# Big on-chip buffers at multiples of 512 bytes, and a matrix of ones kept as one column

## What is computed

```python
def swiglu(h, w_gate, w_up, w_down):
    return (jax.nn.silu(h @ w_gate) * (h @ w_up)) @ w_down

for l in range(DEPTH):                       # first model
    h = rmsnorm(x, norm_mix[l])
    x = x + (even_mixer(h, ...) if l % 2 == 0 else odd_mixer(h, ...))
    h = rmsnorm(x, norm_ffn[l])
    x = x + swiglu(h, ffn_w_gate[l], ffn_w_up[l], ffn_w_down[l])
for l in range(DEPTH):                       # second model
    x = layer_norm(alpha * x + 0.5 * swiglu_2(x, w_ff1_in[l], w_ff1_out[l]), ...)
    mix = hybrid_mixer(x, ...)               # three attention branches and gates
    x = layer_norm(alpha * x + mix, ...)
    x = layer_norm(alpha * x + 0.5 * swiglu_2(x, w_ff2_in[l], w_ff2_out[l]), ...)
```

## Time and profile before

| | us |
|---|---|
| median of 3 runs (2305.82 to 2306.01) | 2305.96 |
| the profiled execution | 2305.82 |
| its span, first to last instruction | 2304.0 |
| PE busy | 2285.6 |
| DVE busy | 1783.4 |
| ACT busy | 1286.9 |

### The profile page before, as it was taken

The page is one execution under the profiler, slowest core; times in us unless marked ns, Lnnn a source line. Parts: engine busy times, 40 slices in busy tenths (PEclk is TensorE's granted clock), DMA queues, the critical chain, the costliest instruction groups (busy, mean ns, idle before and its releaser), DMA issues.

```text
span 2304.0 us, 37657 instructions
## 1 busy us (share of the span) xinstructions
PE 2285.6 (99%) x15127; PEld 2064.6 (90%) x15127; DVE 1783.4 (77%) x2709; ACT 1286.9 (56%) x2017; POOL 80.0 (3%) x96
## 2 busy tenths in 40 slices
PE   8999999999999999999999999999999999999998
PEld 7988889998888888999999888988889999998887
DVE  6989658779858876797679886698767976798854
ACT  6855455655445554585656554455445856565542
POOL 0022000002100000020000000000000200000000
PEclk9999999999999999999999999999999999999999
DMA  6455565456556556554455555566565543556563
GB/s 229 139 189 191 189 210 169 150 162 205 181 176 211 192 185 192 199 181 134 120 182 185 192 189 180 178 192 202 184 195 192 185 138 120 178 183 214 187 182 99
DMA packets 115452, 412.45 MB, mean 179 GB/s; under 512 B 12880, under 2 KB 14800, under 8 KB 115024
## 3 DMA queue, kind: packets, MB, share of 16 engines
q1 hardware_dynamic: 114992, 407.96, 54.5%
q0 software_dynamic: 288, 2.10, 0.3%
HBM read 408.96 MB, written 1.05 MB: 178 GB/s over the span
## 4 chain that ended last, share of the span: by engine, by line
PE 95%; DVE 4%; ACT 1%; issue 1%; DMA 0%; SPq 0%; DVEq 0%; ACTq 0%
PE ps L441 93%; DVE wlo L2015 1%; PE ps L714 0%; DMA raw<-in_ew_c 0%; DVE RX L2207 0%; DVE x L2067 0%; PE ps L962 0%; ACT region L1476 0%; DVE x L2214 0%; ACT whi L1255 0%; PE ps L1078 0%; DVE R L2225 0%; DVE x L2167 0%; DVE R L2194 0%; DVE x L2266 0%
## 5 line engine op out<-in xcount | busy, mean ns | idle before, releaser
L441 PE MATMUL ps<-xx,whi 128*128 128x512 f32 (+1 forms) x4504 | 1218.1, 357 | 3.6 <-DVE wlo L2015 1.8
L2015 DVE TENSOR_TENSOR wlo<-raw,whi 128x1024 fp32r<-128x1024 f32 (+3 forms) x772 | 925.6, 1207 | 270.7 <-ACT whi L1255 269.3
L1255 ACT ACTIVATE whi<-raw 128x1024 fp32r<-128x1024 f32 (+3 forms) x772 | 801.2, 1044 | 534.9 <-PE ps L441 521.8
L441 PEld LDWEIGHTS ps<-xx,wlo 128*128 128x128 f32 x3696 | 696.5, 188 | 127.4 <-DVE wlo L2015 0.2
L441 PE MATMUL ps<-xx,wlo 128*128 128x256 f32 x3696 | 796.9, 279 | 0.0
L441 PEld LDWEIGHTS ps<-xx,whi 128*128 128x128 f32 x4504 | 696.9, 189 | 8.9 <-issue 4.9
L441 PE MATMUL ps<-H,whi 128*128 128x512 f32 (+1 forms) x2144 | 538.2, 339 | 0.4 <-DVE H L2038 0.4
L441 PE MATMUL ps<-H,wlo 128*128 128x256 f32 x1632 | 363.8, 279 | 0.0
L441 PEld LDWEIGHTS ps<-H,wlo 128*128 128x128 f32 x1632 | 306.5, 188 | 46.8
L441 PEld LDWEIGHTS ps<-H,whi 128*128 128x128 f32 x2144 | 329.3, 188 | 1.8 <-issue 1.1
L2010 DVE TENSOR_REDUCE t<-ps 128x256 f32<-128x512 f32 x320 | 219.6, 688 | 46.5 <-PE ps L441 39.8
(11 more groups left out here) (311 smaller groups left out, 1560.7 us busy)
## 6 DMA issues: line engine op xcount, KB each, us to landing
raw<-in_sg SPq DMA_DIRECT2D x128, 512.0 KB, 3.5
raw<-in_su SPq DMA_DIRECT2D x128, 512.0 KB, 3.5
raw<-in_sd SPq DMA_DIRECT2D x128, 512.0 KB, 3.9
raw<-in_mw_g SPq DMA_DIRECT2D x48, 512.0 KB, 3.5
raw<-in_fg SPq DMA_DIRECT2D x44, 512.0 KB, 3.4
raw<-in_fu SPq DMA_DIRECT2D x44, 512.0 KB, 3.2
raw<-in_fd SPq DMA_DIRECT2D x32, 512.0 KB, 3.5
raw<-in_mw_a SPq DMA_DIRECT2D x24, 512.0 KB, 3.9
```

Of the source, the lines that this page charges most:

```text
L441: return e.matmul(out, lhsT, rhs, start=start, stop=stop, skip_group_check=True)
L1255: e.activation(m.whi[:, c % NHL, 0:cw], m.raw[:, c % NRAW, 0:cw], ACT.Copy).then_inc(s["whi"].h, s["whi"].up(c))
L2015: e.tensor_tensor(m.wlo[:, c % NHL, 0:cw], m.raw[:, c % NRAW, 0:cw], m.whi[:, c % NHL, 0:cw].bitcast(F32), ALU.subtract).then_inc(s["wlo"] ...
```

## The change

The small buffers (`pk`, `rowc`, `lvm`, `epsc`, `junk`, `wgb`, `cst`, `R`, the ones) are allocated first. The matrix of 1/1024 becomes one column, 4 bytes in each partition, that is read with a step of zero wherever the matrix was read; it is written by a memset and a copy of one column. A helper, `line`, fills up to the next multiple of 512 bytes, and each big buffer begins there. By the same sum as above `raw` comes to 27136, `whi` to 51712, `wlo` to 72192, `x` to 92672, `xx` to 100864, `t12` to 117248, `H` to 125952, `RX` to 191488 and `arena` to 142336: all at 0 past a multiple of 512. From `raw` to `t12` all move by the same 10624 bytes, so their distances from each other stay. The distance from `whi` to `H` goes from 85056 bytes (64 past a multiple of 512) to 74240 (a multiple of 512). No instruction is added, removed or moved, and no wait changes.

```diff
+    def line(past=0):
+
+        gap = (past - nc.sbuf_base) % 512
+        if gap:
+            sb(f"gap{nc.sbuf_base}", [128, gap // 4])
+        return nc.sbuf_base
+
+    m.pk = sb("pk", [128, NPACK])
+    m.rowc = sb("rowc", [128, 704])
...
+    m.cst = sb("cst", [128, 768])
+    m.R = sb("R", [128, 2, 256])
+    on = -(-nc.sbuf_base // 64) * 64
+    sb("ones_mean", [128, (on - nc.sbuf_base) // 4 + 16])
+    m.one = nc.alloc_sbuf_tensor_at("one", [128, 1], F32, offset=on, align_bytes=64)[:, :]
+    m.onc = nc.alloc_sbuf_tensor_at("onc", [128, 1], F32R, offset=on, align_bytes=64)[:, :]
+    m.onr = m.onc.broadcast_to([128, 128])
+    m.onm = m.onc.bitcast(F32).broadcast_to([128, 128])
+    line(0)
     m.raw = sb("raw", [128, NRAW, CW])
+    line(0)
     m.whi = sb("whi", [128, NHL, CW], F32R)
+    line(0)
     m.wlo = sb("wlo", [128, NHL, CW], F32R)
+    line(0)
     m.x = sb("x", [128, 8, 256])
+    line(0)
     m.xx = sb("xx", [128, 8, 2, 256], F32R)
     m.xh, m.xl = m.xx[:, :, 0, :], m.xx[:, :, 1, :]
-    at = -(-nc.sbuf_base // 64) * 64
-    t12 = sb("t12", [128, 2048 + 128 + 16])
+    at = line(0)
+    t12 = sb("t12", [128, 2048 + 128])
...
-    m.R = sb("R", [128, 2, 256])
-    m.pk = sb("pk", [128, NPACK])
-    m.cst = sb("cst", [128, 768])
...
-    sb("ones_mean", [128, 128 + 16])
-    m.one = nc.alloc_sbuf_tensor_at("one", [128, 128], F32, offset=on, align_bytes=64)[:, :]
-    m.onr = nc.alloc_sbuf_tensor_at("onr", [128, 128], F32R, offset=on, align_bytes=64)[:, :]
-    m.onm = m.onr.bitcast(F32)
...
+    at = line(0)
     left = nc.sbuf_bytes_remaining
-    nar = (left() if callable(left) else left) // 4 - 40 - 4096
-    nar = min(nar, 21696)
-    at = nc.sbuf_base
-    at = -(-at // 64) * 64
-    region = sb("region", [128, 4096 + nar + 16])
+    nar = min((left() if callable(left) else left) // 4 - 8 - 4096, 21696)
+    region = sb("region", [128, 4096 + nar])
     m.H = nc.alloc_sbuf_tensor_at("H", [128, 32, 2, 256], F32R, offset=at, align_bytes=64)
     m.RX = nc.alloc_sbuf_tensor_at("RX", [128, 8, 2, 258], F32R, offset=at + 65536, align_bytes=64)
...
-    arena = region[:, 4112:]
+    arena = region[:, 4096:]
...
-    c = Carve(arena, nar, at=16432)
+    c = Carve(arena, nar, at=16416)
...
-    e.tensor_copy(m.onr, m.one).then_inc(s["set"].h, s["set"].up("onm"))
+    e.tensor_copy(m.onc, m.one).then_inc(s["set"].h, s["set"].up("onm"))
```

More of the change, by code:

```diff
@@ L245, in sb @@
         return ctx.enter_context(nc.sbuf_tensor(name, shape, dt))
+    def line(past=0):
[5 more added lines that the diff above has]
+    m.rowc = sb("rowc", [128, 704])
+    m.lvm = sb("lvm", [128, 5, 128], U8)
+    m.epsc = sb("epsc", [128, 5])
+    junk = sb("junk", [128, 2])
+    m.junk, m.junk0 = junk[:, 0:1], junk[:, 1:2]
+    m.wgb = sb("wgb", [128, 6, 2])
+    m.cst = sb("cst", [128, 768])
[7 more added lines that the diff above has]
+    line(0)
     m.raw = sb("raw", [128, NRAW, CW])
+    line(0)
     m.whi = sb("whi", [128, NHL, CW], F32R)
+    line(0)
     m.wlo = sb("wlo", [128, NHL, CW], F32R)
+    line(0)
     m.x = sb("x", [128, 8, 256])
+    line(0)
     m.xx = sb("xx", [128, 8, 2, 256], F32R)
     m.xh, m.xl = m.xx[:, :, 0, :], m.xx[:, :, 1, :]
-    at = -(-nc.sbuf_base // 64) * 64
-    t12 = sb("t12", [128, 2048 + 128 + 16])
+    at = line(0)
+    t12 = sb("t12", [128, 2048 + 128])
     m.t1, m.t2 = (t12[:, 1024 * i:1024 * i + 1024].rearrange("p (a b) -> p a b", b=256) for i in range(2))
@@ L259, in lay_memory @@
     m.Ph, m.Pl = blk[:, NBLK - 128:NBLK], blk[:, NBLK:NBLK + 128]
-    m.R = sb("R", [128, 2, 256])
-    m.pk = sb("pk", [128, NPACK])
-    m.cst = sb("cst", [128, 768])
[L263 to L268, removed]
-    sb("ones_mean", [128, 128 + 16])
-    m.one = nc.alloc_sbuf_tensor_at("one", [128, 128], F32, offset=on, align_bytes=64)[:, :]
-    m.onr = nc.alloc_sbuf_tensor_at("onr", [128, 128], F32R, offset=on, align_bytes=64)[:, :]
-    m.onm = m.onr.bitcast(F32)
-    m.wgb = sb("wgb", [128, 6, 2])
-    left = nc.sbuf_bytes_remaining
-    nar = (left() if callable(left) else left) // 4 - 40 - 4096
-    nar = min(nar, 21696)
-    at = nc.sbuf_base
-    at = -(-at // 64) * 64
-    region = sb("region", [128, 4096 + nar + 16])
+    at = line(0)
+    left = nc.sbuf_bytes_remaining
+    nar = min((left() if callable(left) else left) // 4 - 8 - 4096, 21696)
+    region = sb("region", [128, 4096 + nar])
     m.H = nc.alloc_sbuf_tensor_at("H", [128, 32, 2, 256], F32R, offset=at, align_bytes=64)
```

## The result

The changed kernel takes 2308.91 us (median of 20 runs, 2308.81 to 2309.16), the kernel before 2305.90 in the same comparison: a ratio of 1.0013, 95% interval 1.0007 to 1.0019. The profiled execution took 2308.94 us, its span 2307.1. So the change costs 3.0 us, 0.13%: within the 0.2% that the prediction set as its limit for no change, and 1.4 us under its forecast of 2310.3.

The account below looks back on a forecast made before the run. PE's matmul stream was taken as the bound, 95% of the chain. Terms on `H`, 4.0 + 3.4 - 2.7 = +4.7 us of PE, became +4.5; 2305.82 + 4.5 = 2310.3 us, range 2265 to 2326.

Parts of the forecast that it names:

- The bound: What limits the whole kernel: PE, busy 2285.6 of 2304.0 us and 95% of the chain that ended last.
- The ones, the loads, ACT and DVE at nothing: One-column ones, moved landing buffer for outside loads, and moved ACT and DVE operands: each priced at 0 us.
- The stream on `xx` at nothing: PE matmuls streaming `xx` past `whi` and `wlo`: distance to the weights stays, so 0 us.
- The stream on `H`: PE matmuls on `H` take the pace of `xx`: wide products +4.0 us, products in three +3.4, token-major -2.7.
- Token-major: 408 PE matmuls of 512 columns with `H` stationary: 233.3 to 226.7 ns each, -2.7 us.
- `RX`: 240 triples streaming `RX` on PE, rows at all sorts of places: 0, bound 1.6 us either side.
- The sum: PE terms on `H`, 4.0 + 3.4 - 2.7 = +4.7 us; with PE 95% of the chain, +4.5 us.
- The factor of 0.95: PE's 95% share of the chain, used to turn +4.7 us of PE into +4.5 us of kernel time.
- Faster through the offset itself: Rival: operands at a 512-byte multiple touch fewer lines, all PE streams gain; 2288.4 to 2254 us, middle about 2271; chance 0.32.
- Slower since aligned reads meet more: Rival, wide products on `xx`: aligned tile and row meet twice as often, 2880 pairs pay 4.9 ns; 2323.7 us; chance 0.13.
- Nothing: Rival: `xx` and `H` differ by loops or other address bits, PE shows no change; 2305.8 us; chance 0.15.
- The rule of 16-byte lines: Skill's rule that each crossing to a new SBUF line costs: crossings stay equal, PE unchanged, 2305.8 us.

## Why the prediction was right

*The bound.* PE at 95% of the chain; after, 96%. Right.

*The ones, the loads, ACT and DVE at nothing.* The ones were run alone and gave no difference. DMA stays at 0% of the chain, DVE was busy 1.3 us more and ACT 0.2, and the sum by streams leaves 0.3 us for all that is not `H` or `RX`.

*The stream on `xx` at nothing.* 696.8 and 360.0 ns after 696.4 and 360.0. Right, and for the reason given: the distance stayed. Between the two kernels `xx` went from 128 to 0 past a multiple of 512, and to 192 in the run with all at 192, at the same pace; with the weights moved it changed its pace without moving.

*The stream on `H`.* Forecast +4.0 wide and +3.4 in three, 7.4 together; measured +7.1. Token-major forecast -2.7, measured -2.7. `RX` was taken at 0 with a bound of 1.6 on either side; it gave 0.9. That is the term that was mis-sized: its rows of 1032 bytes lie at other distances now. That these are better on the average is argued; the run with `H` and `RX` back at 64 shows that the 0.9 us go with the distance.

*The sum.* 7.08 - 2.67 - 0.88 - 0.31 = 3.22 us between the first and last start, 3.0 in the medians, where +4.5 was forecast: `RX` is 0.9 of the difference, `H` and the other work about 0.3 each. The factor of 0.95 played no part that can be told from these small terms. That the time lies in a range 61 us wide says little; the prediction is borne out by the paces it named for `H`, 696, 360 and 227 ns, and for `xx`, each met to about 1 ns.

*The rivals.* Faster through the offset itself: out (`xx` at 128, 0 and 192). Slower since aligned reads meet more: `xx` did not change. Nothing: out, since `H` did change; the time alone, at 0.13%, would not have told these apart, the paces did. The rule of 16-byte lines (the Trainium skill, "SBUF — State Buffer", "Door 1: The DMA port swizzle") gives the same pace wherever buffers begin at multiples of 16, since the lines crossed are as many; the runs do not agree, with 690 and 707 ns at distances of 64 and 96. The Trainium skill also states that loading the next weights takes no read bandwidth from the running matmul ("TensorE: Matmul & The Clock Gate", "Step-by-step: what each phase is for"). That does not fit either: with the activations in place, moving the weights alone took the wide cycle on `xx` from 697 to 690 ns.

What no run shows is the mechanism below this: whether the two reads meet in a bank, a line buffer or elsewhere.

## What to carry to other kernels

Where PE is busy all the time, look at the pace of equal streams and not at the busy share: two buffers whose streams differ by a per cent point to where they lie. What counts is the distance between the streaming and the stationary buffer, so rounding everything to the same multiple is no neutral choice: here it brought distance 0, slower than 64 for `H` as the stream, though the fastest for token-major. Some bytes of padding, chosen by a few runs, gave 0.5% over the kernel before.

## What was not expected of the hardware

- With float32r operands the pace of a stream varies with the distance to the weights: 690 to 707 ns for a wide cycle, 340 to 362 ns for a triple. A period of 256 bytes fits the wide and token-major paces; the triples leave it open.
- The fastest steady paces seen are 226.7 ns for 512 columns and 340.0 / 3 = 113.3 ns for 256, both 17/16 of the 213.3 and 106.7 ns that the columns would take at one a clock of 2.4 GHz. No distance tried gave less.
- The same stream at the same addresses can keep either of two rhythms (353.3 and 340.0 ns a triple, 703.3 and 693.2 ns a wide cycle). What picks one is not shown: in two kernels it changed behind one matmul in between, in the kernel before the same matmul changed nothing, and with the ones alone changed a stretch of 31 triples took the other rhythm. Whether a matmul in between can start the faster one at will was not tried.
